# One decoder layer on one core: two groups of narrow matrix products issued as pairs in the two column halves of the TensorE array

## The chip, the cores and the metric

The kernel is one program on one core of one Trainium2 chip. The metric is the device time of one execution in microseconds. Before the change it is 1077.32 us, the median of three runs (1077.20 to 1079.56). All data and products are float32.

## What is computed

The reference is one hybrid decoder layer on x (256 tokens x 1024). What matters here is the compressed branch of the attention and the place where probabilities meet values:

```
# token mixer: one input projection; then attention (3 branches) beside a convolution branch
blocks = concat of two neighbouring chunks of 16 tokens, + pos_emb      # 15 blocks per group, 4 groups
kc = gelu(blocks.reshape(.., 32*96) @ w1k) @ w2k                        # w1k: 3072 x 256
vc = gelu(blocks.reshape(.., 32*64) @ w1v) @ w2v                        # w1v: 2048 x 256
o_cmp = softmax(q @ kc.T * scale + bias, masked) @ vc                   # 16 heads, value width 64
o_slc = softmax(q @ ks.T * scale + bias, causal) @ vs                   # all 4 blocks are selected
o_win = softmax(q @ kw.T * scale + bias, causal) @ vw
o = g0*o_cmp + g1*o_slc + g2*o_win                                      # -> w_attn_out, merged, w_out
# then PEER: q = h @ w_q; scores against sub-keys; top 16 of 128 x 128 experts for each of 8 heads;
# y = sum_e gelu(h . u[e]) * w_e * v[e]      (128 experts a token, rows u,v gathered from memory)
```

## The kernel before, in words

The program has one instruction stream per engine, written out by hand in the order of work; semaphores tie the streams together. TensorE executes its stream in order. Its stages are:

1. Input projection: `column_tile` multiplies 128x128 weight tiles by hT (channels x 256 tokens), 8 products per tile of output columns.
2. Block compression. Keys lie as kcA and kcB (first and second half of a block with position embedding; 96 rows of one position and 32 rows of another packed into 128 partitions) in `sc`, values as vcAB. For each of 24 steps the stationary operand is a slice of every 16th column of kcA or kcB (63 columns, one for each block of the four groups; NCG = 63) and the moving operand is a 128x256 slice of w1. All steps accumulate into `pb[0:63, 5, 0:256]`. ScalarE applies gelu into htok (63 x 256), and `hidden_transposed` turns it by two transposes into 128 x 63 twice. The values do the same in 16 steps into bank 7. In between and after stand the second layer products (w2k, w2v) and the first two tiles of the convolution's output projection (`conv_out`).
3. Attention: 32 units n, one for each of 2 token tiles (tt = 0, 1) and 16 heads. In each iteration TensorE runs `scores(n)`, some products of the convolution branch (`conv_pieces`, only while tt = 0), `transposes(n-2)` of the probabilities, and one piece of `values` of the group of four heads gi that was finished before; at every fourth iteration also `cmp_scores` and `cmp_transposes`. VectorE runs `logits(n)`, then `gated(n-1)`; ScalarE the exponentials and the copy of the turned probabilities into PT.
4. `values(gi, piece)`: the output of four heads lies in `o = pb[0:64, 6 + gi % 2, 0:512]` (64 value channels x 4 heads x 128 tokens). Piece 0 multiplies the compressed values vcv (15 rows x 64 columns) by PcT (15 x 512); the other products multiply V (128 x 64) by PT (128 x 512). With tt = 0 there are 1 + 2 products for a group, with tt = 1 there are 1 + 4. These are 8 products at L704 and 24 at L709. `attention_out(gi)` on ScalarE copies even heads to partitions 0-63 of hT and odd heads to partitions 64-127, with two instructions that each read 64 partitions, and each raises a_o by 1.
5. After the attention: `attention_out_half` (products by w_attn_out), `out_part` (by w_out), norms, the first query columns and sub-key scores, and the search for the first experts on VectorE.
6. Experts: GpSimd issues indirect DMAs of 256 rows a token tile and expert (1 MB each) at L516 as `rowat` places come free; VectorE forms the dot products (L1479), TensorE adds diag x row into PSUM (`expert_chunk`, L794). The last additions and the store end the program.

Each float32 product appears in the trace as two records of TensorE, each with its own weight load (PEld).

Of the kernel before, what the change touches and what calls it, by code (L numbers as in the profile page):

```python
# [26 lines left out]
ACT = mybir.ActivationFunctionType  # L27
AX = mybir.AxisListType.X

P = 128  # L30
# [3 lines left out]
TT = SEQ // P  # L34
HEADS = 16
GROUPS = 4
REP = HEADS // GROUPS
DQK = 96
DV = 64
CMP_L = 32  # L40
CMP_ST = 16
NCMP = SEQ // CMP_ST - 1
NBLK = SEQ // CMP_ST
NFAR = (P - CMP_L) // CMP_ST + 1
NCG = GROUPS * NBLK - 1
HID = 256
# [31 lines left out]
KAT = 8  # L78
# [111 lines left out]
def build(nc, a, out):  # L190
    ctx = ExitStack()
    with ctx:
        def sb(name, shape, dt=F32):
            return ctx.enter_context(nc.sbuf_tensor(name, shape, dt))

        def sem(name):
            return ctx.enter_context(nc.semaphore(name))
# [9 lines left out]
        w1 = arena[:, 4:12, :].rearrange("p a b -> p (a b)").rearrange("p (l n) -> p l n", n=HID)  # L207

        x = sb("x", [P, TT, D])
        hT = sb("hT", [P, DT, SEQ])  # L210
# [6 lines left out]
        V = sb("V", [P, TT, 2 * GROUPS * DV])  # L217
# [10 lines left out]
        sc = sb("sc", [P, 4096])  # L228
# [14 lines left out]


        kcA, kcB, vcAB = (sc[:, 1024 * i:1024 * i + 1024] for i in range(3))
        ssb = sc[:, :].rearrange("p (t m k) -> p t m k", t=TT, k=NK)
        pair = sb("pair", [P, 2 * D])
        S = pair[:, :].rearrange("p (u b t) -> p u b t", u=4, b=2)
# [5 lines left out]
        PT = arena[:, 4:8, :].rearrange("p a b -> p (a b)").rearrange("p (u k t) -> p u k t", u=2, t=512)  # L254
        scaled = [sc[:, 1024:2048], sc[:, 1024:2048]]
        spare = sb("spare", [P, 2 * D])
        PcT = spare[:, 1024:2048].rearrange("p (u t) -> p u t", u=2)
        htok = spare[0:NCG, 0:512].rearrange("p (u n) -> p u n", u=2)
        tbc = spare[:, 512:512 + TT * HEADS * NCMP].rearrange("p (t h n) -> p t h n", t=TT, h=HEADS)

        rowat = [qk[:, 3 * D:5 * D]]
# [17 lines left out]
        table = sb("table", [BUCKETS + 1, HEADS])  # L279
# [7 lines left out]
        vcv = sb("vcv", [NCMP, GROUPS * DV])  # L287
# [8 lines left out]
        ident = sb("ident", [P, P])  # L296
# [29 lines left out]
        pb = ctx.enter_context(nc.psum_tensor("pb", [P, 8, 512], F32))  # L326
# [15 lines left out]
        v_sc, v_p, v_pc, a_o = sem("v_sc"), sem("v_p"), sem("v_pc"), sem("a_o")  # L342
        g_const, g_rowok, g_chain = sem("g_const"), sem("g_rowok"), sem("g_chain")
        a_c, a_ss, a_std, a_rev = (sem(n) for n in ("a_c", "a_ss", "a_std", "a_rev"))
        a_evac, a_v, a_gk, a_hk, a_kc, a_gv, a_hv, a_vc, a_stdc, a_z = (
            sem(n) for n in ("a_evac", "a_v", "a_gk", "a_hk", "a_kc", "a_gv", "a_hv", "a_vc", "a_stdc", "a_z"))
# [28 lines left out]
        def group_of(gi):  # L375

            return divmod(gi, GROUPS)
# [145 lines left out]
        def _(pe):  # L523
            mm = nc.tensor.matmul
# [4 lines left out]
            for hf in range(2):  # L529
                last = mm(pb[:, hf, :], ones[0:1, :], crow[:, hf * 512:(hf + 1) * 512], start=True, stop=True)  # L530
# [3 lines left out]
            for j in range(DT):  # L534
                if j == 4:
                    pe.wait_ge(v_xs, TT)
                    for t in range(TT):
                        last = mm(pb[:, 2, t * P:(t + 1) * P], ones[:, :], turn[:, t, :], start=True, stop=True)
                    last.then_inc(p_xT, 1)
                for t in range(TT):  # L540
                    o = (j % 2) * SEQ + t * P
                    last = nc.tensor.transpose(pb[:, 4 + j // 2, o:o + P], x[:, t, j * P:(j + 1) * P], ident[:, :])
# [22 lines left out]
            for k in range(DT):  # L565
                pe.wait_ge(ring_in[k], 16)
                pe.wait_ge(a_hT, k + 1)
                for n in range(ROUND):
                    if k == 0 and n >= 6:
                        pe.wait_ge(a_xh, n - 2)  # L570
                    last = mm(pb[:, n, 0:SEQ], ring[:, k, n * P:(n + 1) * P], hT[:, k, :],
                              start=(k == 0), stop=(k == DT - 1))
# [34 lines left out]
            pe.wait_ge(a_pack, 6)  # L607
            for n in range(3 * CMP_L // 4):
                l = n // 3 * 4 + n % 3
                src = kcA if l < CMP_ST else kcB  # L610
                last = mm(pb[0:NCG, 5, 0:HID], src[:, l:l + (NCG - 1) * CMP_ST + 1:CMP_ST], w1[:, KAT + n, :],
                          start=(n == 0), stop=(n == 3 * CMP_L // 4 - 1))
                if n == KAT - 1:
                    last.then_inc(p_hk, 1)
            last.then_inc(p_hk, 1)
            def hidden_transposed(u, bank):
                for hh in range(2):
                    last = nc.tensor.transpose(pb[:, bank, hh * 64:hh * 64 + NCG], htok[:, u, hh * P:(hh + 1) * P],
                                               ident[0:NCG, 0:NCG])
                return last  # L620

            pe.wait_ge(a_gk, 1)
            hidden_transposed(0, 6).then_inc(p_tk, 1)

            pe.wait_ge(w1v_in, 32)
            for l in range(CMP_ST):
                last = mm(pb[0:NCG, 7, 0:HID], vcAB[:, l:l + (NCG - 1) * CMP_ST + 1:CMP_ST], w1[:, l, :],
                          start=(l == 0), stop=(l == CMP_ST - 1))
            last.then_inc(p_hv, 1)
            pe.wait_ge(a_hk, 1)  # L630
            pe.wait_ge(s_small, 64)
            for k in range(2):
                last = mm(pb[0:DQK, 6, 256:256 + NCG], w2k[:, k, :], hidk[:, k, 0:NCG], start=(k == 0), stop=(k == 1))
# [12 lines left out]
            for g in range(GROUPS):  # L646
                for k in range(2):
                    last = mm(pb[0:NCMP, 5, 256 + g * DV:256 + (g + 1) * DV], hidv[:, k, g * NBLK:g * NBLK + NCMP],
                              w2v[:, k, :], start=(k == 0), stop=(k == 1))
# [6 lines left out]
            def cmp_scores(gi):  # L656
                tt, g = group_of(gi)
                if gi >= 3:
                    pe.wait_ge(a_o, 2 * (gi - 2))
                for hh in range(REP):  # L660
                    last = mm(pb[:, 6 + (gi + 1) % 2, hh * NCMP:(hh + 1) * NCMP], qT[0:DQK, g * REP + hh, tt * P:(tt + 1) * P],
                              kcT[:, g * NBLK:g * NBLK + NCMP], start=True, stop=True)
                last.then_inc(p_cs, 1)
# [11 lines left out]
            def scores(n):  # L675
                tt, h, g, hh, keys = unit_keys(n)
                if n >= 2:
                    pe.wait_ge(v_mx, 2 * (n - 1))
                mm(pb[:, n % 2, 0:2 * keys], qT[0:DQK, h, tt * P:(tt + 1) * P], kT[0:DQK, g, 1:3, 0:keys],  # L679
                   start=True, stop=True).then_inc(p_s, 1)  # L680
# [14 lines left out]

            def values(gi, piece):
                tt, g = group_of(gi)
                o = pb[0:DV, 6 + gi % 2, :]
                if piece == 0:
                    pe.wait_ge(a_pct, gi + 1)  # L700
                    if gi >= 2:
                        pe.wait_ge(a_o, 2 * (gi - 1))
                    pe.wait_ge(v_cs, min(gi + 2, GROUPS * TT))
                    mm(o, vcv[:, g * DV:(g + 1) * DV], PcT[0:NCMP, gi % 2, :], start=True, stop=False)  # L704
                pe.wait_ge(a_pt, REP * (gi + 1))
                products = [(b, kb) for b in range(2) for kb in range(tt + 1)]
                mine = products[piece:piece + 1] if tt else products[piece - 1:piece] if piece else []
                for b, kb in mine:
                    last = mm(o, V[:, kb, (b * GROUPS + g) * DV:(b * GROUPS + g + 1) * DV],  # L709
                              PT[:, gi % 2, b * (tt + 1) + kb, :], start=False, stop=((b, kb) == products[-1]))  # L710
                    if (b, kb) == products[-1]:
                        last.then_inc(p_o, 1)

# [23 lines left out]
            for n in range(NU + 2):  # L737
                if n < NU:
                    if n % REP == 0:
                        cmp_scores(n // REP)  # L740
                    scores(n)
                conv_pieces(n)
                if n >= 2:
                    transposes(n - 2)
                if n < NU and n % REP == 2:
                    cmp_transposes(n // REP)
                if n >= REP + 2:
                    values((n - REP - 2) // REP, (n - REP - 2) % REP)
                if n == NU:
                    pe.wait_ge(a_o, 2 * GROUPS)  # L750
                    pe.wait_ge(v_zb, DT)
                    attention_out_half(0, 0)
                    attention_out_half(0, 1)
                if n == NU + 1:
                    pe.wait_ge(v_mx, 2 * NU)
                    attention_out_half(0, 2)
# [71 lines left out]
            for hf in range(2):  # L828
                for k in range(DT):
                    last = out_part(0, k, (hf,))  # L830
                last.then_inc(p_out, 1)
            pe.wait_ge(a_o, 2 * GROUPS * TT)
            for j in range(3):
                attention_out_half(1, j)
            h2_transposes(0)
# [36 lines left out]
        def _(act):  # L872
            fn = nc.scalar.activation
# [70 lines left out]
            fn(stdc[:, :], pb[:, 4, SEQ:2 * SEQ], ACT.Sqrt, bias=eps[:, :]).then_inc(a_stdc, 1)  # L944
            fn(turned[:, :], eps[:, :], ACT.Gelu_apprx_tanh).then_inc(a_turn, 1)
            act.wait_ge(p_hk, 2)
            fn(htok[:, 0, :], pb[0:NCG, 5, 0:HID], ACT.Gelu_apprx_tanh).then_inc(a_gk, 1)
            act.wait_ge(p_tk, 1)
            fn(hidk[:, :, 0:NCG], pb[:, 6, 0:P].rearrange("p (a b) -> p a b", a=2)[:, :, 0:NCG],
               ACT.Copy).then_inc(a_hk, 1)  # L950
# [4 lines left out]
            act.wait_ge(p_kc, 1)  # L955
            fn(kcT[:, :], pb[0:DQK, 6, 256:256 + NCG], ACT.Copy).then_inc(a_kc, 1)
            act.wait_ge(p_hv, 1)
            fn(htok[:, 1, :], pb[0:NCG, 7, 0:HID], ACT.Gelu_apprx_tanh).then_inc(a_gv, 1)
            act.wait_ge(p_tv, 1)
            fn(hidv[:, :, 0:NCG], pb[:, 5, 0:P].rearrange("p (a b) -> p a b", a=2)[:, :, 0:NCG],  # L960
               ACT.Copy).then_inc(a_hv, 1)
# [20 lines left out]
            def attention_out(gi):  # L982
                tt, g = group_of(gi)
                act.wait_ge(p_o, gi + 1)
                o = pb[0:DV, 6 + gi % 2, :].rearrange("p (a b t) -> p a b t", b=2, t=P)
                for odd in range(2):
                    fn(hT[odd * DV:(odd + 1) * DV, 2 * g:2 * g + 2, tt * P:(tt + 1) * P], o[:, :, odd, :],
                       ACT.Copy).then_inc(a_o, 1)

            for n in range(NU + 2):  # L990
                gi = n // REP
# [677 lines left out]
```

## Time and profile before

| what | value |
|---|---|
| median of three runs | 1077.32 us |
| span of the profiled execution (first to last instruction) | 1074.3 us |
| part of the median outside that span | 3.0 us |
| PE busy / DVE / ACT / POOL | 954.7 / 732.4 / 297.0 / 337.1 us |
| queue of the indirect DMAs | 292.59 MB, 67.0% of 16 engines' span |
| mean rate over the span | 336 GB/s |

The profile gives no time for its own execution beside the span; 1074.3 us of span stand against 1077.32 us of median, so 3.0 us lie around the span (start and end of the program), and differences of span are read as differences of time. Busy shares are averages over stages with different limits; the stretches in the rows below separate the stages. In a timeline, the first number is the start of a group of instructions, the second the time it was busy, and "x" the number of records.

### The profile page before, as it was taken

Reading aid. Unit: us, or ns where it says so; the run is one execution under the profiler, and the core shown is the slowest. Engines: PE = TensorE matmul, PEld = TensorE weight load, DVE = VectorE, ACT = ScalarE, POOL = GpSimd, SP = SyncE. Lnnn points to the kernel's source line nnn. Section 1 sums busy time; section 2 is a strip of 40 time slices with the busy share of each in tenths; the row PEclk is TensorE's granted clock in tenths of the full one; section 3 lists DMA queues with packets and bytes.
Section 4 is the critical chain, followed back from the end, with each engine's and each line's share of the span. In section 5 each row is a group of like instructions: output and inputs, shape, how many; then the busy total and the mean of one; then the engine's idle time right before and its main releaser. Section 6 shows DMA issues by size and latency. Waiting matters only on the chain.

```text
span 1074.3 us, 11042 instructions
## 1 busy us (share of the span) xinstructions
PE 954.7 (89%) x3303; PEld 567.7 (53%) x3303; DVE 732.4 (68%) x1933; ACT 297.0 (28%) x811; POOL 337.1 (31%) x325
## 2 busy tenths in 40 slices
PE   7999999999999999899999878787778777778786
PEld 5788888887644675565565433333333323333332
DVE  6699798734456149768748667767678667667554
ACT  3211122254456121523312312212322212212222
POOL 0101003021000015445435644455444454444430
PEclk9999999999999999999999987999889999999899
DMA  9967748886100809999999999999999999999994
GB/s 364 403 248 224 266 150 333 333 306 132 59 20 6 339 32 409 423 384 423 421 422 422 420 423 421 423 424 421 423 423 422 422 423 423 422 423 423 422 423 172
DMA packets 63290, 361.91 MB, mean 337 GB/s; under 512 B 7500, under 2 KB 8156, under 8 KB 30078
## 3 DMA queue, kind: packets, MB, share of 16 engines
q0 software_dynamic: 43280, 292.59, 67.0%
q1 hardware_dynamic: 19950, 68.61, 17.2%
q8 instruction: 27, 0.44, 0.2%
q14 instruction: 33, 0.27, 0.1%
HBM read 359.58 MB, written 1.59 MB: 336 GB/s over the span
## 4 chain that ended last, share of the span: by engine, by line
PE 49%; DMA 35%; DVE 8%; ACT 2%; POOL 2%; issue 2%; SPq 2%; ACTq 0%; POOLq 0%; DVEq 0%
DMA arena<-in_peer_uv,idx 21%; PE pb L553 18%; PE pb L794 14%; DMA ring<-in_peer_uv,idx 10%; DMA qk<-in_peer_uv,idx 2%; PE pb L709 2%; PE pb L679 2%; PE pb L722 2%; PE pb L732 2%; DVE arena L1479 2%; DMA arena<-in_w_ada 2%; PE pb L587 1%; PE pb L774 1%; POOL arena L516 1%; PE pb L823 1%
## 5 line engine op out<-in xcount | busy, mean ns | idle before, releaser
L794 PE MATMUL pb<-arena,sig 128*128 128x512 f32 x416 | 193.3, 616 | 22.4 <-ACT sig L1071 22.4
L794 PE MATMUL pb<-ring,sig 128*128 128x512 f32 x288 | 140.3, 633 | 29.4 <-ACT sig L1071 29.4
L553 PE MATMUL pb<-hT,ring 128*128 128x256 f32 x752 | 162.8, 379 | 0.5 <-ACT arena L899 0.5
L516 POOL DMA_INDIRECT arena<-in_peer_uv,idx x104 | 123.1, 1183 | 113.2 <-PE pb L794 93.1
L1479 DVE CUSTOM_DVE_ANT_0 arena<-arena,sig 128x1024 f32<-128x1024 f32 x104 | 124.4, 1223 | 44.6 <-DMA arena<-in_peer_uv,idx 44.1
L553 PEld LDWEIGHTS pb<-hT,ring 128*128 128x128 f32 x752 | 142.7, 190 | 21.1 <-ACT arena L899 1.7
L794 PEld LDWEIGHTS pb<-arena,sig 128*128 128x128 f32 x416 | 80.9, 197 | 128.9 <-issue 128.7
L1068 ACT ACTIVATE gl<-dot 128x4 f32<-128x4 f32 (+1 forms) x73 | 14.9, 205 | 413.4 <-DVE dot L1479 397.1
L516 POOL DMA_INDIRECT ring<-in_peer_uv,idx x72 | 88.2, 1225 | 91.8 <-PE pb L794 82.4
L1479 DVE CUSTOM_DVE_ANT_0 ring<-ring,sig 128x1024 f32<-128x1024 f32 x72 | 87.7, 1224 | 40.9 <-DMA ring<-in_peer_uv,idx 40.4
L794 PEld LDWEIGHTS pb<-ring,sig 128*128 128x128 f32 x288 | 56.9, 203 | 105.8 <-issue 105.7
L794 PE MATMUL pb<-qk,sig 128*128 128x512 f32 x160 | 81.5, 648 | 27.4 <-ACT sig L1071 27.3
L1199 DVE SCALAR_TENSOR_TENSOR y<-arena,cols,y x240 | 95.2, 474 | 0.0
L1071 ACT ACTIVATE sig<-ident,cf 128x128 f32<-128x128 f32 x256 | 82.8, 390 | 16.8 <-DVE cf L1483 16.8
L516 POOL DMA_INDIRECT qk<-in_peer_uv,idx x40 | 47.0, 1176 | 117.9 <-PE pb L794 64.7
L463 POOL DMA_DIRECT2D arena<-in_w_ada x32 | 17.1, 541 | 167.5 <-DVE modst L1147 131.3
L1479 DVE CUSTOM_DVE_ANT_0 qk<-qk,sig 128x1024 f32<-128x1024 f32 x40 | 49.4, 1235 | 28.8 <-DMA qk<-in_peer_uv,idx 28.2
L794 PEld LDWEIGHTS pb<-qk,sig 128*128 128x128 f32 x160 | 31.0, 201 | 69.5 <-issue 69.3
L1290 DVE CUSTOM_DVE_ANT_0 pair<-pb,arena 128x128 f32<-128x128 f32 (+1 forms) x64 | 20.3, 355 | 37.2 <-PE pb L679 34.8
L794 PE MATMUL pb<-pair,sig 128*128 128x512 f32 x44 | 26.2, 727 | 20.5 <-ACT sig L1071 20.5
L1147 DVE CUSTOM_DVE_ANT_0 arena<-arena,sc 128x1024 f32<-128x1024 f32 x32 | 37.9, 1223 | 8.9 <-DMA arena<-in_w_ada 8.3
L794 PE MATMUL pb<-hT,sig 128*128 128x512 f32 x72 | 38.3, 658 | 0.4 <-ACT sig L1071 0.4
(313 smaller groups left out, 1263.0 us busy)
## 6 DMA issues: line engine op xcount, KB each, us to landing
ring<-in_w_stream SPq DMA_DIRECT2D x79, 512.0 KB, 7.2
arena<-in_w_ada POOLq DMA_DIRECT2D x32, 512.0 KB, 11.7
arena<-in_w_ada SPq DMA_DIRECT2D x12, 512.0 KB, 11.7
arena<-in_w_stream SPq DMA_DIRECT2D x8, 512.0 KB, 6.6
arena<-in_w1k SPq DMA_DIRECT2D x6, 512.0 KB, 8.6
spare<-in_w_stream SPq DMA_DIRECT2D x6, 512.0 KB, 8.5
pair<-in_w_stream SPq DMA_DIRECT2D x5, 512.0 KB
sig<-in_w_ada SPq DMA_DIRECT2D x4, 512.0 KB, 14.8
```

Of the source, the lines that this page charges most:

```text
L516: nc.gpsimd.indirect_dma_start(out=rowat[PLACE[n]], out_offset=None, in_=a["peer_uv"], in_offset=bass.IndirectOffsetOnAxis(ap=idx[:, c, e: ...
L553: last = mm(pb[:, bank, 0:SEQ], w[:, k * P:(k + 1) * P], src[:, k, :], start=(k == 0), stop=(k == DT - 1))
L679: mm(pb[:, n % 2, 0:2 * keys], qT[0:DQK, h, tt * P:(tt + 1) * P], kT[0:DQK, g, 1:3, 0:keys], start=True, stop=True).then_inc(p_s, 1)
L709: last = mm(o, V[:, kb, (b * GROUPS + g) * DV:(b * GROUPS + g + 1) * DV], PT[:, gi % 2, b * (tt + 1) + kb, :], start=False, stop=((b, kb) ...
L722: last = mm(pb[:, MERGE_BANK[q], side * P:(side + 1) * P], tile_at[SLOT[tile]][:, k * P:(k + 1) * P], hT[:, k, t * P:(t + 1) * P], start=( ...
L732: last = mm(pb[:, 4, 0:SEQ], ring[:, SLOT[T_CO + j], k * P:(k + 1) * P], y[:, k, :], start=(k == 0), stop=(k == DT - 1))
L794: last = mm(pb[:, 4 + 2 * t + hf, :], diag[:, c % DEEP, e, :], rowat[PLACE[n]][:, D + hf * 512:D + (hf + 1) * 512], start=(i == 0 and e == ...
L1071: fn(diag[:, b, s, :], ident[:, :], ACT.Copy, scale=cf[:, b, s:s + 1]).then_inc(a_dg, 1)
L1147: V_.tensor_tensor_reduce(out=w[:, s, :], in0=w[:, s, :], in1=cact, scale=1.0, scalar=0.0, op0=ALU.mult, op1=ALU.add, accum_out=modst[:, s ...
L1199: ins = V_.scalar_tensor_tensor(out=y[:, j, :], in0=upad[:, j, k:k + SEQ], scalar=w, in1=y[:, j, :], op0=ALU.mult, op1=ALU.add)
L1290: V_.tensor_tensor_reduce(out=S[:, n % 4, b, 0:keys], in0=pb[:, n % 2, b * keys:(b + 1) * keys], in1=tb[:, h, SEQ - keys:SEQ], scale=-SCAL ...
L1479: V_.tensor_tensor_reduce(out=u, in0=u, in1=h2[:, c // CPT, :], scale=1.0, scalar=0.0, op0=ALU.mult, op1=ALU.add, accum_out=dot[:, c % DEE ...
```

## The change

The products of the two places become pairs. Compression: the slice takes 64 columns instead of 63, and each step becomes two products, one with the first 128 columns of w1 into partitions 0-63 and one with the last 128 into partitions 64-127 of the same bank, columns 0-127. The gelu then reads 128 x 128, and the hidden layer is turned by one transpose instead of two. Values: every product of 64 x 512 becomes two of 64 x 256, even heads into partitions 0-63 and odd heads into 64-127, and ScalarE copies them out with one instruction of 128 partitions; the waits on a_o count half as many.

```diff
+        kcBv = sc[:, 1024:3072]
-        htok = spare[0:NCG, 0:512].rearrange("p (u n) -> p u n", u=2)
+        htok = spare[:, 0:256].rearrange("p (u n) -> p u n", u=2)
...
-                src = kcA if l < CMP_ST else kcB
-                last = mm(pb[0:NCG, 5, 0:HID], src[:, l:l + (NCG - 1) * CMP_ST + 1:CMP_ST], w1[:, KAT + n, :],
-                          start=(n == 0), stop=(n == 3 * CMP_L // 4 - 1))
+                src = kcA if l < CMP_ST else kcBv
+                for hh in range(2):
+                    last = mm(pb[hh * 64:hh * 64 + 64, 5, 0:P], src[:, l:l + 63 * CMP_ST + 1:CMP_ST],
+                              w1[:, KAT + n, hh * P:(hh + 1) * P], start=(n == 0), stop=(n == 3 * CMP_L // 4 - 1))
...
             def hidden_transposed(u, bank):
-                for hh in range(2):
-                    last = nc.tensor.transpose(pb[:, bank, hh * 64:hh * 64 + NCG], htok[:, u, hh * P:(hh + 1) * P],
-                                               ident[0:NCG, 0:NCG])
-                return last
+                return nc.tensor.transpose(pb[:, bank, 0:P], htok[:, u, :], ident[:, :])
...
             for l in range(CMP_ST):
-                last = mm(pb[0:NCG, 7, 0:HID], vcAB[:, l:l + (NCG - 1) * CMP_ST + 1:CMP_ST], w1[:, l, :],
-                          start=(l == 0), stop=(l == CMP_ST - 1))
+                for hh in range(2):
+                    last = mm(pb[hh * 64:hh * 64 + 64, 7, 0:P], vcAB[:, l:l + 63 * CMP_ST + 1:CMP_ST],
+                              w1[:, l, hh * P:(hh + 1) * P], start=(l == 0), stop=(l == CMP_ST - 1))
...
             def values(gi, piece):
                 tt, g = group_of(gi)
-                o = pb[0:DV, 6 + gi % 2, :]
+                def sides(v, table, first, final):
+                    for odd in range(2):
+                        last = mm(pb[odd * DV:(odd + 1) * DV, 6 + gi % 2, 0:2 * P].rearrange("p (a t) -> p a t", t=P), v,
+                                  table.rearrange("k (a b t) -> k a b t", b=2, t=P)[:, :, odd, :], start=first, stop=final)
+                    return last
...
-                    mm(o, vcv[:, g * DV:(g + 1) * DV], PcT[0:NCMP, gi % 2, :], start=True, stop=False)
+                    sides(vcv[:, g * DV:(g + 1) * DV], PcT[0:NCMP, gi % 2, :], True, False)
...
-                    last = mm(o, V[:, kb, (b * GROUPS + g) * DV:(b * GROUPS + g + 1) * DV],
-                              PT[:, gi % 2, b * (tt + 1) + kb, :], start=False, stop=((b, kb) == products[-1]))
+                    last = sides(V[:, kb, (b * GROUPS + g) * DV:(b * GROUPS + g + 1) * DV],
+                                 PT[:, gi % 2, b * (tt + 1) + kb, :], False, (b, kb) == products[-1])
...
-            fn(htok[:, 0, :], pb[0:NCG, 5, 0:HID], ACT.Gelu_apprx_tanh).then_inc(a_gk, 1)
+            fn(htok[:, 0, :], pb[:, 5, 0:P], ACT.Gelu_apprx_tanh).then_inc(a_gk, 1)
...
             def attention_out(gi):
-                o = pb[0:DV, 6 + gi % 2, :].rearrange("p (a b t) -> p a b t", b=2, t=P)
-                for odd in range(2):
-                    fn(hT[odd * DV:(odd + 1) * DV, 2 * g:2 * g + 2, tt * P:(tt + 1) * P], o[:, :, odd, :],
-                       ACT.Copy).then_inc(a_o, 1)
+                fn(hT[:, 2 * g:2 * g + 2, tt * P:(tt + 1) * P],
+                   pb[:, 6 + gi % 2, 0:2 * P].rearrange("p (a t) -> p a t", t=P), ACT.Copy).then_inc(a_o, 1)
```

## Rows read from the trace of the kernel before

**Rows 1.** The page's chain that ended last, by engine.

```profile
PE 49%; DMA 35%; DVE 8%; ACT 2%; POOL 2%; issue 2%; SPq 2%; ACTq 0%; POOLq 0%; DVEq 0%
```

**Rows 2.** Busy time by stretch, attention to end, with granted clock and DMA share.

```profile
core 0: us, PE busy (x) PEld busy (x) DVE busy (x) ACT busy (x) POOL busy (x), PEclk, DMA share, GB/s
253.00:299.00 46.00, 43.97 (x210) 31.89 (x210) 25.07 (x144) 22.82 (x89) 0.00 (x0) 1.00 0.26 82
299.00:349.10 50.10, 48.50 (x186) 21.22 (x184) 31.19 (x144) 30.66 (x98) 2.04 (x4) 1.00 0.05 13
349.10:363.60 14.50, 14.50 (x83) 9.23 (x82) 1.98 (x5) 2.04 (x5) 0.15 (x1) 1.00 0.83 319
363.60:412.00 48.40, 48.05 (x285) 35.92 (x285) 22.39 (x76) 11.13 (x26) 6.25 (x7) 1.00 0.48 183
412.00:530.00 118.00, 113.99 (x445) 68.87 (x444) 89.75 (x241) 37.23 (x101) 56.52 (x46) 1.00 1.01 414
530.00:1074.00 544.00, 440.73 (x986) 193.70 (x984) 372.04 (x920) 130.44 (x356) 243.61 (x205) 0.93 0.98 410
```

**Rows 3.** What PE waited for from 224 to 412 us (total, times, longest).

```profile
PE pb L732 <- DVE arena L1254: 2.0, 2, 1.0
PE pb L692 <- DVE pair L1303: 1.3, 3, 0.6
```

**Rows 4.** Timeline of PE around one isolated product of the values.

```profile
302.46 0.38 PE L692 MATMUL pb<-ident,pair 128*128 128x128 f32 x2
302.77 1.07 PE L709 MATMUL pb<-arena,V 128*64 128x512 f32 x2
303.77 1.12 PE L679 MATMUL pb<-qk 96*128 96x512 f32 x2
```

**Rows 5.** Timeline at the end of the values: a stream of products.

```profile
359.05 1.07 PE L704 MATMUL pb<-spare,vcv 15*64 15x512 f32 x2
360.04 3.65 PE L709 MATMUL pb<-arena,V 128*64 128x512 f32 x8
363.62 7.41 PE L722 MATMUL pb<-hT,ring 128*128 128x128 f32 x64
```

**Rows 6.** The weight loads of the same stream.

```profile
360.04 0.19 PEld L709 LDWEIGHTS pb<-arena,V 128*64 128x64 f32 x2 [0.81 <-issue]
360.52 0.14 PEld L709 LDWEIGHTS pb<-arena,V 128*64 128x64 f32 x1 [0.29 <-issue]
363.62 0.97 PEld L722 LDWEIGHTS pb<-hT,ring 128*128 128x128 f32 x8 [0.81 <-issue]
```

**Rows 7.** Key compression (L611): weight loads and products, min/median/max ns.

```profile
L611 PEld LDWEIGHTS pb<-arena,sc x48: 183/184/205, 224.9 to 234.9; 128*63 128x63 f32 x48
L611 PE MATMUL pb<-arena,sc x48: 379/379/480, 224.9 to 235.1; 128*63 128x256 f32 x48
```

**Rows 8.** Timeline from the key compression to the value compression and on.

```profile
235.55 0.38 ACT L947 ACTIVATE spare<-pb 63x256 f32<-63x256 f32 x1 [6.27 <-PE pb L611]
235.98 0.33 PE L618 MATMUL pb<-ident,spare 63*128 63x63 f32 x2 [0.47 <-ACT spare L947]
236.24 7.17 PE L627 MATMUL pb<-arena,sc 128*63 128x256 f32 x32
243.34 0.55 PE L633 MATMUL pb<-hidk,w2k 128*96 128x63 f32 x4
```

**Rows 9.** Streams of short records: 15, 128 and 64 moving columns.

```profile
251.25 1.07 PE L648 MATMUL pb<-w2v,hidv 128*15 128x64 f32 x16
252.25 1.06 PE L661 MATMUL pb<-kcT,qk 96*128 96x15 f32 x8
300.60 1.06 PE L661 MATMUL pb<-kcT,qk 96*128 96x15 f32 x8
301.51 1.10 PE L679 MATMUL pb<-qk 96*128 96x512 f32 x2
350.07 3.84 PE L722 MATMUL pb<-hT,ring 128*128 128x128 f32 x32
353.75 0.60 PE L692 MATMUL pb<-ident,pair 128*128 128x128 f32 x4
```

**Rows 10.** One iteration with tt = 1: scores, gating on VectorE, transposes.

```profile
326.89 1.12 PE L679 MATMUL pb<-qk 96*128 96x512 f32 x2
328.94 0.73 DVE L1303 TENSOR_SCALAR pair<-pair,rz,gates 128x256 f32<-128x256 f32 x2
329.38 1.12 PE L679 MATMUL pb<-qk 96*128 96x512 f32 x2
330.35 0.60 PE L692 MATMUL pb<-ident,pair 128*128 128x128 f32 x4
```

**Rows 11.** ScalarE's copies in the attention, by shape: busy, mean ns, idle before.

```profile
L979 ACT ACTIVATE arena<-pb 128x256 f32<-128x256 f32 x16 | 6.0, 372 | 5.1 <-PE pb L692 5.1
L987 ACT ACTIVATE hT<-pb 64x256 f32<-64x256 f32 x16 | 5.9, 371 | 8.2 <-PE pb L709 8.0
```

More of the change, by code:

```diff
@@ L658, in cmp_scores @@
                 if gi >= 3:
-                    pe.wait_ge(a_o, 2 * (gi - 2))
+                    pe.wait_ge(a_o, gi - 2)
                 for hh in range(REP):
@@ L701, in values @@
                     if gi >= 2:
-                        pe.wait_ge(a_o, 2 * (gi - 1))
+                        pe.wait_ge(a_o, gi - 1)
                     pe.wait_ge(v_cs, min(gi + 2, GROUPS * TT))
-                    mm(o, vcv[:, g * DV:(g + 1) * DV], PcT[0:NCMP, gi % 2, :], start=True, stop=False)
+                    sides(vcv[:, g * DV:(g + 1) * DV], PcT[0:NCMP, gi % 2, :], True, False)
                 pe.wait_ge(a_pt, REP * (gi + 1))
@@ L749, in _ @@
                 if n == NU:
-                    pe.wait_ge(a_o, 2 * GROUPS)
+                    pe.wait_ge(a_o, GROUPS)
                     pe.wait_ge(v_zb, DT)
@@ L831, in _ @@
                 last.then_inc(p_out, 1)
-            pe.wait_ge(a_o, 2 * GROUPS * TT)
+            pe.wait_ge(a_o, GROUPS * TT)
             for j in range(3):
@@ L957, in _ @@
             act.wait_ge(p_hv, 1)
-            fn(htok[:, 1, :], pb[0:NCG, 7, 0:HID], ACT.Gelu_apprx_tanh).then_inc(a_gv, 1)
+            fn(htok[:, 1, :], pb[:, 7, 0:P], ACT.Gelu_apprx_tanh).then_inc(a_gv, 1)
             act.wait_ge(p_tv, 1)
```

## The prediction

> **What bounds the kernel now.** I read the chain of work that ended last first: half of it is PE and a third DMA [rows 1], so there are stages with different limits. The busy times by stretch separate them [rows 2]. Up to 412 us PE is the limit: it is busy 43.97 of 46.00 us, 48.50 of 50.10, 14.50 of 14.50 and 48.05 of 48.40, while DVE and ACT reach about 60% at most. The reader is to see that the DMA share there is 0.05 to 0.83. From 412 us on the DMA share is 1.01 and then 0.98, at 414 and 410 GB/s: the expert rows are gathered at full rate to the end. The gather can't become shorter by this change, but it begins when the PE stages ahead of it end. A microsecond that PE saves ahead of 412 us moves the whole gather forward by one, and one that it loses moves it back. Both edited places lie ahead of it, and PE hardly waits there: 2.0 us in all for the convolution merges and 1.3 us for the gated probabilities [rows 3].
>
> **How long one product takes now.** The records end with a tail that overlaps the next, so I use start to start. The isolated product of the values goes from 302.77 to 303.77 [rows 4]: 1.00 us for two records of 512 moving columns. In the stream at the end, 8 such records take 363.62 - 360.04 = 3.58 us [rows 5]. Two equations, 2r + s = 1.00 and 8r + s = 3.58, give r = 0.430 us a record and s = 0.14 us for entering or leaving the shape of 64 weight columns. The weight loads show what s is: inside the stream the next weights load while the current record runs (one load at 360.52, between the records), but the first load at 360.04 and that of the following 128-column product at 363.62 begin only with their own record, after 0.81 us of idle [rows 6]. So the array is already driven in a 64-column shape there, and changing the shape drains it. The change keeps the shape (64 weight columns), so s is paid as often as before. A record of 256 moving columns takes half of 0.430, 0.215 us; the compression's own rows agree, 10.2 us for 47 steps from its first to its last record, 0.217 us [rows 7].
>
> **Values.** There are 32 products (8 + 24). The last four of L709 are one stream; the 28 others are isolated, each between other shapes: the product of vcv has 15 rows and that of V 128, and from 359.05 to 360.04 the change between these two costs the same 0.99 us a product [rows 5]. After the change each product is four records of 0.215 us: A1, A2 into partitions 0-63 and B1, B2 into 64-127.
> - If the halves of the array don't work at the same time, a pair costs 4 x 0.215 + 0.14 = 1.00 us: nothing gained.
> - If they do, the stream is still in order: A2 must follow A1 in its half, B1 can start beside A2, B2 follows B1. An isolated pair then costs 3 x 0.215 + 0.14 = 0.785 us, 0.215 less. In a stream each further pair costs two records, so the last four take 9 x 0.215 + 0.14 = 2.08 us in place of 3.58, 1.50 less.
> Together 28 x 0.215 + 1.50 = 7.5 us. No row of before shows two column halves in use at once; the bounds are 7.5 us gained and, if each change of half costs a drain, 35 changes (28 in isolated pairs, 7 in the stream) x 0.14 = 4.9 us lost. If B's weights load late, with the 0.14 us uncovered, an isolated pair gains 0.075 and the whole about 2.1 + 0.5 = 2.6 us. I take 7.5, since the two weight loads that come together at 360.04 (0.19 us for both) show loads fast enough to run ahead of records of 0.215 us.
>
> The Trainium skill (TensorEngine Tiling, "Key Properties") says that tiles run independently and that changing the tiling mode, not the tile, drains the engine. The drains at shape changes in the trace agree with the second half; no row here shows the first. The same skill (TensorE: Matmul & The Clock Gate, "Packing small matmuls") says that a weight load overlaps a running product only when the row group differs; here the trace disagrees, since the load at 360.52 runs under a product of the same rows, and the measurement decides. By that rule alone the values would gain nothing and the time would be that of the second rival below, 1077.7 us; the tiling page's rule gives the forecast.
>
> How much of it passes through: with tt = 1 the scores of an iteration follow those of the one before by 329.38 - 326.89 = 2.49 us, and the gated probabilities are ready at 328.94 + 0.73 = 329.67 while their transposes start at 330.35 [rows 10]. With 0.14 us for the weight load that leaves about 0.5 us of cover, more than the 0.215 taken from the iteration. In the iterations without a value piece PE waits already, and they gain nothing, but they have nothing to lose either. I pass 95%: 7.1 us. If the cover were gone, the loss would show as more wait at L692.
>
> **Compression.** Before: 24 key steps of two records. After: 96 records of 128 moving columns, each with a load of 64 weight columns taken at every 16th column. Those loads are slow: 183 ns for 63 columns [rows 7], where V's 64 neighbouring columns take about 0.14 us in the rows of the stream [rows 6]. Loads of 128 columns bind the stream of L661, whose moving operand is only 15 columns: 8 records from 300.60 to 301.51, 0.114 us each [rows 9]. L722, with 128 moving and 128 weight columns, needs 3.68 us for 32, 0.115 us [rows 9]. So I expect 0.108 to 0.115 us a record whether or not the products overlap, because the loads follow one another: 96 x 0.112 = 10.75 us against 48 x 0.217 = 10.4 now, 0.3 lost, and 64 x 0.112 = 7.2 against 32 x 0.217 = 6.9 in the value compression [rows 8], 0.2 lost. Bounds: if loads of different halves run side by side, two records of 0.108 make a pair's time and it gains half: 5.2 + 3.5 = 8.7 us less at most. If each change of half drains, 47 + 31 changes x 0.14 = 10.9 us more. I take +0.5, nearest to the two rows of streams with short records.
>
> **Small parts.** The gelu of the keys stands in PE's way: 0.38 us for 63 x 256, then PE starts at 235.98, having waited 0.47 [rows 8]. Half the free size makes it some 0.1 us shorter; one transpose in place of two about 0.05 (236.24 - 235.98 = 0.26 for both now). That of the values is hidden by `conv_out`. ACT's copies out of the values become one of 128 x 256 instead of two of 64 x 256; a 128-partition copy of that size takes 372 ns and each of 64 partitions 371 [rows 11], so 8 x 0.37 = 3.0 us of ACT go. ACT has slack there (30.66 of 50.10 us [rows 2]), so 0. The waits on a_o come at the same points. No DMA is added or moved; those that start on p_hk and p_o start that much earlier or later with PE.
>
> **Sum.** -7.1 + 0.5 - 0.15 = -6.8 us. Span 1074.3 - 6.8 = 1067.5; with the 3.0 us between the span and the median of the runs 1070.5 us.
>
> **The rivals.**
> - Both overlap, loads too. For it: nothing in the rows ties the loads of one half to the other. Against: each of PE's loads in the rows stands behind the one before. Time: a pair of compression records is unlikely to reach the bound of 8.7 us fully; at the 0.063 us a record that the shortest stream of the values' second layer needs (16 records from 251.25 to 252.25 us [rows 9]) it is 96 x 0.063 = 6.0 and 64 x 0.063 = 4.0, so 4.4 + 2.9 = 7.3 less. With the values 7.1 and 0.15: -14.5, 1062.8 us.
> - The change doesn't do what it says: float32 products of the two halves run one after the other. For it: every record in the trace follows the one before with no overlap in the array. Values 0, compression +0.5, small -0.15: 1077.7 us, up to 1078.6 if a record there takes 0.12 us.
> - The other side: every change of the column half drains as a change of shape does, 0.14 us. For it: the exposed loads of [rows 6]. Against: what changes there is the number of columns, not only where they are. It decides from the first pair on. 4.9 + 10.9 + 0.5 - 0.15 = +16.1: 1093.5 us; if it does so only in the values or with half the price, 1082 to 1086.
>
> **How the numbers follow.** Forecast (values overlap, compression bound by loads) 0.40, with 1069 to 1075 as its own range; both overlap 0.20; no overlap 0.26; drains 0.14. Less than 0.3% (3.2 us) can't be told from no change here. Faster: 0.20 + 0.37 of the forecast's 0.40 = 0.57. Same: 0.03 + 0.23 = 0.26. Slower: 0.14 + 0.03 = 0.17. The range reaches from the second case to the serial one and a part of the drains: 1061 to 1080.5.
>
> **What would show it.** In the profile after, the starts of L709's successor: a pair of four records with 128x256 should take 0.79 us to the next shape's start, 1.00 if serial, 1.14 if it drains. The last stream before L722 should take 2.1 us. The key compression should take 10.4 to 11.0 us from first to last record; 6 us would show parallel loads, 17 us drains. L692's waits should stay below 3 us in all. From 412 us on the stages should be only shifted: DMA share 0.98 and over. If the PE stages end earlier and the end doesn't move, the gather was bound to something else, and that would make the prediction wrong.

## The result

The changed kernel takes 1063.76 us, the median of four runs (1061.19 to 1066.58), against 1077.26 us; the ratio is 0.9871, 95% interval 0.9846 to 0.9896, or 13.5 us less. A second series of runs of it gave 1063.99 us and 0.9876 (0.9861 to 0.9891). I had forecast 1070.5 us, 6.8 less. The sign was right, the size half of the measured one, and two of the steps were wrong in opposite directions.

The profiled execution has a span of 1064.8 us, 9.5 less than the 1074.3 before, and its time, 1066.58 us, is the longest of the first four. The span gained 4.0 us less than the median. In every run with a time and a span of its own on record the time is 1.7 to 1.9 us more than the span, so the profiled execution before took about 1076.1 us (an estimate, 1074.3 + 1.8), 1.2 less than its median, and the profiled one after took 2.8 more than its median: 13.5 - 1.2 - 2.8 = 9.5. These are the milestones of the two traces:

| start of | before | after | gained since the row above |
|---|---|---|---|
| key compression (L611, now L613) | 224.89 | 226.75 | -1.86 |
| its transposes (L618, L619) | 235.98 | 232.95 | 4.89 |
| value compression (L627) | 236.24 | 240.85 | -7.64 |
| second layer of the keys (L633) | 243.34 | 246.11 | 1.84 |
| first scores of the attention (L661) | 252.25 | 254.66 | 0.36 |
| products after the last values (L722, L729) | 363.62 | 353.79 | 12.24 |
| w_out (L774, L781) | 370.87 | 361.04 | 0.00 |
| end of the span | 1074.3 | 1064.8 | -0.3 |

The code ahead of the first row is the same in both. In the traces of this case the key compression starts anywhere from 224.8 to 228.1 us, so the 1.86 us are not put down to the change; what they come from is open. Everything from the last values on is only shifted. The lengths of stages, compared over all traces at the end of the experiments, don't suffer from the different starts.

**Values.** This is PE's timeline of the changed kernel around the same isolated product as in [rows 4]; L702 now stands for L704 and L709.

```profile
301.52 0.38 PE L692 MATMUL pb<-ident,pair 128*128 128x128 f32 x2
301.83 0.65 PE L702 MATMUL pb<-arena,V 128*64 128x256 f32 x4
302.41 1.13 PE L679 MATMUL pb<-qk 96*128 96x512 f32 x2
```

From 301.83 to 302.41 the pair takes 0.58 us, where the product took 1.00. Two record times of 0.215 and the drain of 0.14 make 0.57: four records in the time of two. The same pair, cut to what started before 302.00, and its weight loads:

```profile
301.83 0.44 PE L702 MATMUL pb<-arena,V 128*64 128x256 f32 x2
```
```profile
301.83 0.20 PEld L702 LDWEIGHTS pb<-arena,V 128*64 128x64 f32 x4 [0.17 <-issue]
```

Two records are there, and together they are busy for 0.44 us, about as long as one of them alone (up to 430 ns, the first of a stream has the longest tail). The rows don't name the half of a record. But two records of one half follow each other by a record time (experiment 3), so the two that start together are A1 and B1, not A1 and A2. All four weight loads are done in 0.20 us. The stream at the end, against [rows 5]:

```profile
351.33 0.65 PE L702 MATMUL pb<-spare,vcv 15*64 15x256 f32 x4
351.91 1.95 PE L702 MATMUL pb<-arena,V 128*64 128x256 f32 x16
353.79 7.41 PE L729 MATMUL pb<-hT,ring 128*128 128x128 f32 x64
```

16 records take 1.88 us (before: 8 records, 3.58).

**Compression.** Timeline of PE, and the durations of the key compression's records (min/median/max ns), against [rows 7, 8]:

```profile
226.75 5.82 PE L613 MATMUL pb<-arena,sc 128*64 128x128 f32 x96
232.95 0.33 PE L619 MATMUL pb<-ident,spare 128*128 128x128 f32 x1 [0.38 <-ACT spare L954]
240.85 5.32 PE L627 MATMUL pb<-arena,sc 128*64 128x128 f32 x64 [7.58 <-DMA arena<-in_w1v]
246.11 0.55 PE L633 MATMUL pb<-hidk,w2k 128*96 128x63 f32 x4
```
```profile
L613 PEld LDWEIGHTS pb<-arena,sc x96: 188/198/221, 226.7 to 232.2; 128*64 128x64 f32 x96
L613 PE MATMUL pb<-arena,sc x96: 274/277/380, 226.7 to 232.3; 128*64 128x128 f32 x96
```

96 records in 5.8 us, 0.060 us each. The slow loads last 198 ns each, a little more than the 184 of [rows 7], and yet one is done every 0.060 us: the loads of the two halves run side by side as well. But then PE waits 7.58 us for the second half of w1v. GpSimd's timeline and the stretches (the last three numbers are granted clock, DMA share, GB/s) show why:

```profile
229.20 0.53 POOL L471 DMA_DIRECT2D arena<-in_w1v  x1 [16.57 <-PE pb L613]
233.20 8.41 POOL L477 DMA_DIRECT2D arena<-rev_scratch  x16 [3.47 <-PE pb L613]
```
```profile
229.00:233.00 4.00, 3.62 (x64) 3.43 (x61) 3.31 (x2) 2.38 (x5) 0.53 (x1) 1.00 1.04 420
233.00:241.00 8.00, 0.42 (x3) 0.23 (x5) 0.88 (x2) 5.60 (x10) 7.80 (x15) 0.76 1.03 215
241.00:246.00 5.00, 5.00 (x64) 4.99 (x64) 0.00 (x0) 0.00 (x0) 0.60 (x2) 0.70 1.05 161
```

The transfer is issued when the first 8 key steps free their place, at 229.20; it lands 11.6 us later, at about 240.8. From 233.20 on GpSimd issues the 16 copies of the bias table, and in the stretch that follows the DMA share stays at 1.03 while the rate falls from 420 to 215 GB/s. Before it was issued at 228.9, landed after 6.5 us at 235.4, and was used at 236.24: 0.8 us of slack that I had not looked for. While PE idles the granted clock falls, to 0.76 and 0.70 in the mean of these stretches, which mix full and half speed (2.4 and 1.2 GHz); the value compression begins in it and takes 5.3 us; in experiment 4, with no wait and at the full clock, it takes 4.0.

**The rest.** What PE waited for from 224 to 412 us, against [rows 3], and the gather's stretches, against [rows 2]:

```profile
PE pb L627 <- DMA arena<-in_w1v: 7.6, 1, 7.6
PE pb L739 <- DVE arena L1259: 2.0, 2, 1.0
PE pb L692 <- DVE pair L1308: 2.0, 3, 0.8
```
```profile
404.00:530.00 126.00, 121.99 (x461) 72.90 (x461) 97.12 (x258) 41.01 (x112) 60.37 (x49) 1.00 1.00 413
530.00:1064.00 534.00, 423.93 (x954) 185.13 (x952) 362.75 (x899) 126.64 (x344) 236.07 (x201) 0.94 0.98 410
```

The gather runs at the same rate and is only earlier.

### The profile page after: what moved, and what is told of

Read it like the earlier page. It is cut to its first block, busy times and chain, and to the rows that moved or that the text cites. A ratio compares the mean times of both kernels' runs of the same rounds, so it can differ in the third digit from the quotient of the medians.

```text
span 1064.8 us, 11318 instructions
## 1 busy us (share of the span) xinstructions
PE 928.2 (87%) x3445; PEld 561.7 (53%) x3445; DVE 731.9 (69%) x1933; ACT 293.6 (28%) x803; POOL 335.0 (31%) x325
## 4 chain that ended last, share of the span: by engine, by line
PE 51%; DMA 37%; DVE 6%; ACT 2%; SPq 2%; issue 2%; POOL 1%; POOLq 0%; ACTq 0%; DVEq 0%
DMA arena<-in_peer_uv,idx 19%; PE pb L554 18%; PE pb L801 16%; DMA ring<-in_peer_uv,idx 15%; PE pb L781 3%; PE pb L729 2%; PE pb L739 2%; DMA arena<-in_w_ada 2%; PE pb L679 2%; PE pb L830 2%; DVE arena L1484 1%; PE pb L588 1%; PE pb L702 1%; DMA arena<-in_w1v 1%; DVE ring L1484 1%
## 5 line engine op out<-in xcount | busy, mean ns | idle before, releaser
L801 PE MATMUL pb<-arena,sig 128*128 128x512 f32 x416 | 193.4, 616 | 27.6 <-ACT sig L1076 27.6
L801 PE MATMUL pb<-ring,sig 128*128 128x512 f32 x288 | 137.2, 620 | 30.7 <-ACT sig L1076 30.7
L517 POOL DMA_INDIRECT ring<-in_peer_uv,idx x72 | 85.4, 1186 | 91.8 <-PE pb L801 81.7
L801 PE MATMUL pb<-hT,sig 128*128 128x512 f32 x72 | 35.5, 617 | 0.4 <-ACT sig L1076 0.4
```

The source lines that it names most:

```text
L517: nc.gpsimd.indirect_dma_start(out=rowat[PLACE[n]], out_offset=None, in_=a["peer_uv"], in_offset=bass.IndirectOffsetOnAxis(ap=idx[:, c, e: ...
L801: last = mm(pb[:, 4 + 2 * t + hf, :], diag[:, c % DEEP, e, :], rowat[PLACE[n]][:, D + hf * 512:D + (hf + 1) * 512], start=(i == 0 and e == ...
```

## The experiments

All times are medians against the kernel before on the same chip.

**1. The compression alone as pairs**, values as before (the diff of the change without `values` and `attention_out`).

> Only the compression as pairs, the values as before. Theory (records of the two halves start within some ns of each other, and the weight loads of the two halves run side by side too; the second half of w1v then arrives late and gives part back): key compression from first to last record 5.5 us in place of 10.2, value compression 3.8 to 5.3 in place of 6.8, but PE waits 3 to 8 us for w1v ahead of the latter. Time 0 to 5 us below before. Rival (the gain of the compression is whole and the time in the two is lost nowhere): 7 to 8 us below before.

Measured: 1076.01 against 1077.04 us, ratio 0.9986 (0.9978 to 0.9995), 1.0 us. PE's timeline:

```profile
226.94 5.82 PE L613 MATMUL pb<-arena,sc 128*64 128x128 f32 x96
240.20 5.76 PE L627 MATMUL pb<-arena,sc 128*64 128x128 f32 x64 [6.75 <-DMA arena<-in_w1v]
```

The theory holds for the time: nearly all that the two compressions gain goes into the wait. The value compression takes 5.7 us, more than the 3.8 to 5.3 expected; its first 4.1 us lie at a granted clock of 0.50.

**2. The values alone as pairs**, compression as before.

> Only the values as pairs (and the one copy of 128 partitions), compression as before. Theory: an isolated product takes 0.58 us start to start in place of 1.00, so 28 x 0.42 + 1.7 = 13.4 us less of PE time, some of it turning into waits for VectorE: span of attention 12 us shorter, time 11.5 to 12.5 us below before, and no wait for w1v, since the key compression takes its 10.2 us. Rival (much of the gain of the whole change comes from the compression): 7 us below before.

Measured: 1064.06 us, ratio 0.9877 (0.9862 to 0.9891), 13.0 us, a little more than the theory's 12.5. No wait for w1v. Experiments 1 and 2 add up to 14.0, the whole change gives 13.5: the measured gain is that of the values.

**3. The same narrow products, both of a pair in one half of the array** (abridged; the compression keeps its 63 weight columns).

```diff
-                last = mm(pb[0:NCG, 5, 0:HID], src[...], w1[:, KAT + n, :], ...)
+                for hh in range(2):
+                    last = mm(pb[0:NCG, 5, hh * P:(hh + 1) * P], src[...], w1[:, KAT + n, hh * P:(hh + 1) * P], ...)
...
+                        last = mm(pb[0:DV, 6 + gi % 2, :].rearrange("p (a b t) -> p a b t", b=2, t=P)[:, :, odd, :], v, ...)
```

> The same narrow products (64 weight columns x 128 or 256 moving) in both places, but both of a pair into partitions 0 to 63, side by side in the bank; copies and gelu as before. Theory (the gain is that two halves of the array work at once): no overlap, values 1.00 us a pair as before, compression bound by its slow weight loads at 0.108 to 0.12 us a record, so 10.4 to 11.5 and 7 to 7.7 us; time 0 to 2 us above before. Rival (short records overlap in any place, or a narrower product is cheaper by itself): time 5 to 13 us below before.

Measured: 1077.37 us, ratio 1.0003 (0.9995 to 1.0012). The key compression, and a pair of the values with what follows it:

```profile
228.04 10.76 PE L612 MATMUL pb<-arena,sc 128*63 128x128 f32 x96
...
357.77 1.08 PE L705 MATMUL pb<-arena,V 128*64 128x256 f32 x4
358.77 3.84 PE L733 MATMUL pb<-hT,ring 128*128 128x128 f32 x32
```

The pair takes 1.00 us, the key compression 10.76 and the value compression 7.2. Narrower or shorter records give nothing; it is the second half of the array. The prediction's price of a serial record, 0.112 us, is met here.

**4. w1v early**: the changed kernel, with the second half of w1v loaded into a quarter of `sc` and half of `pair`, both free at that time (GpSimd's part of the edit; TensorE waits for all three transfers and reads the last eight steps from the two places).

```diff
-            g.wait_ge(p_hk, 1)
-            g.dma_start(w1[:, KAT:CMP_ST, :], a["w1v"][:, KAT:CMP_ST, :]).then_inc(w1v_in, 16)
             g.wait_ge(rev_out, 16)
+            for i in range(2):
+                g.dma_start(w1v_late[i], a["w1v"][:, KAT + 4 * i:KAT + 4 * i + 4, :]).then_inc(w1v_in, 16)
```

> The changed kernel with the second half of w1v loaded early into two places that are free (no wait for the first 8 key steps, 2 DMAs of 512 KB in place of one of 1 MB). Theory (the late w1v costs the changed kernel 7.6 us of wait, and some more by the clock that falls to 1.2 GHz in it): no wait ahead of the value compression, which takes 3.8 us or less at the full clock; 7 to 9 us below the changed kernel's profiled span of 1064.8, so 1056 to 1058 of span, 1058 to 1060 of time. Rival (the gather's start is bound by something else behind the attention, or the copies of the bias, which wait for the end of the key compression, come too late in turn): no more than 3 us below 1063.8.

Measured: 1058.40 us (1055.71 to 1059.97), ratio 0.9817 (0.9801 to 0.9834), 18.6 us below before. The whole compression runs through; 96 and 64 records:

```profile
228.00:233.90 5.90, 5.89 (x97) 5.61 (x96) 2.87 (x2) 4.42 (x10) 0.00 (x0) 1.00 1.03 410
234.50:238.40 3.90, 3.90 (x65) 3.85 (x64) 0.79 (x2) 3.75 (x7) 3.90 (x8) 1.00 1.02 266
```

The span, 1056.7 us, is 8.1 below the changed kernel's, as expected; the medians differ by 5.4, since that kernel's profiled execution was 2.8 us above its median. It beats both kernels.

**5. The changed kernel again**, for a second profile. No line of it differs.

> The changed kernel once more, for a second profile: its first runs fell into two groups, 1061.3 and 1066.4 us. Theory (what differs is how late the second half of w1v lands behind the other transfers): the wait ahead of the value compression is 2 to 8 us and differs from the 7.6 us of the first profile by as much as the times do. Rival (the start of the program differs, as the first records of the input projection at 45.6 us against 43.8 in the kernel before suggest): the wait is 7 to 8 us again and the times go with the start of the projection.

Measured: 1063.99 us (1062.31 to 1065.17), ratio 0.9876. The wait was 6.35 us, the landing 10.4; the span was 1063.4, 1.4 shorter. The wait was 1.2 us shorter, but the values' compression took 6.1 us instead of 5.3, more of it at the low clock (5.1 us against 3.2 at 0.50), which gave most of that back. The key compression started 0.5 us earlier (226.26 against 226.75), the first scores 0.9, and the other 0.5 us come behind them. So neither theory is confirmed, and the two groups of the first four runs remain unexplained; here the runs didn't form them.

**6. and 7. How far apart partners may stand.** On top of experiment 4, the order of the compression's products: n products of the first half, then n of the second (one line of the edit; n is RUN_K for the keys and RUN_V for the values). Each was run once: 1058.06 us with runs of 2 and 4, 1071.4 with runs of 24 and 16. In the second the granted clock was 0.50 from 308 to 321 us, in the attention, so its time isn't used; the stages below lie ahead of that.

```diff
+            for hh, n in [(hh, b + i) for b in range(0, 3 * CMP_L // 4, RUN_K) for hh in range(2) for i in range(RUN_K)]:
```

> Kernel of the early w1v, with another order in the compression: two products of the first half, then two of the second (keys), four and four (values' compression). Theory A (each half of the array has its own place in the queue, so that a product finds its partner some products away): keys 5.8 us and values 3.9 us from first to last record, as with alternating products. Theory B (TensorE starts records in the order of the program, and only neighbours overlap): a run of 4 records of the one half overlaps only at its edge, 6 of 8 record times for the keys, 8.1 us, and 14 of 16 for the values, 6.3 us.

> As e6, with all 24 key products of the first half ahead of all 24 of the second, and 16 and 16 for the values. Theory A with a short queue, and theory B: no overlap but at one edge, keys 10.4 to 10.8 us, values 6.9 to 7.3 us, at 0.108 to 0.112 us a record. Theory A with a long queue: 5.8 to 8 us for the keys.

| products in a run | records | us (keys: busy; values: to the next stage's start) |
|---|---|---|
| keys, 1 (changed kernel) | 96 | 5.8 |
| keys, 2 | 96 | 5.9 |
| keys, 24 | 96 | 10.7 |
| values' compression, 1 (experiment 4) | 64 | 4.0 |
| values' compression, 4 | 64 | 5.1 |
| values' compression, 16 | 64 | 7.0 |

Theory A would give 5.8 and 3.9 us in runs of 2 and 4, theory B 8.1 and 6.3; the keys go with A, and the values, at 5.1, lie between the two. TensorE does reach past products of a busy half, but not far. Where the run of 16 changes halves (operand `pair` is the end of the first half, `arena` the start of the second), the second half's first record starts at 242.13, 0.44 us, or four record times, ahead of the point where it runs alone:

```profile
242.13 0.38 PE L630 MATMUL pb<-arena,sc 128*64 128x128 f32 x1
242.23 0.27 PE L630 MATMUL pb<-pair,sc 128*64 128x128 f32 x1
242.34 0.28 PE L630 MATMUL pb<-arena,sc 128*64 128x128 f32 x1
242.34 0.28 PE L630 MATMUL pb<-pair,sc 128*64 128x128 f32 x1
242.45 0.28 PE L630 MATMUL pb<-arena,sc 128*64 128x128 f32 x1
242.46 0.27 PE L630 MATMUL pb<-pair,sc 128*64 128x128 f32 x1
242.57 1.62 PE L630 MATMUL pb<-arena,sc 128*64 128x128 f32 x13
```

Here the operands tell the two halves apart: records of `arena` start ahead of records of `pair` that come before them in the program. The order of the program, which the description of the kernel before took for the order in TensorE, holds within a half.

**8. The kernel before with w1v early.**

> The kernel before, with the second half of w1v loaded early into the free places, nothing else. Theory (before, w1v landed at 235.4 us, 0.8 us ahead of its use, so that it cost nothing): within 0.1% of before. Rival (the early place of the transfer helps by itself, by what it takes out of the way of the bias copies): 2 us or more below before.

Measured: 1077.27 us, ratio 1.0005 (0.9996 to 1.0014). The profiled execution, 1081.65 us, had a granted clock of 0.50 from 310 to 320 us. The early place is worth something only once the compression is fast.

**9. The bias copies only when w1v has landed**: the changed kernel with one line more, so that the 16 copies of small packets don't meet the transfer.

```diff
             g.wait_ge(p_hk, 2)
+            g.wait_ge(w1v_in, 32)
```

> The changed kernel with one more wait: the 16 copies of the bias table (issued from the end of the key compression on, in small packets) are issued only when w1v has landed. In the changed kernel w1v takes 10.4 and 11.6 us to land and PE waits 6.3 and 7.6 us for it. Theory (the copies, now issued 3 us earlier against w1v, share the DMA engines with it and delay it): w1v lands in about 7 us, as the 6.5 us before the change, the wait is 3 to 4 us, and the time is 1060 to 1062 if the bias still comes in time for the first scores. Rival (w1v queues behind the weight tiles that were issued before it, and the copies don't matter): it lands in 10 us or more, the wait is as long as before, and the time 1063 to 1066.

Measured: 1061.52 us (1061.22 to 1061.71), ratio 0.9858 (0.9842 to 0.9874). w1v lands in 7.4 us, and PE waits 3.3:

```profile
236.28 5.51 PE L628 MATMUL pb<-arena,sc 128*64 128x128 f32 x64 [3.31 <-DMA arena<-in_w1v]
```

As the theory had it: of the 6.3 and 7.6 us of wait, some 3 to 4 come from the copies that start earlier and share the engines, and 3.3 are there because the value compression now wants its weights sooner than a transfer issued at 228.9 can bring them. With the wait added the median is about 2 us lower. The intervals of the two ratios overlap, and two of the eight runs of the changed kernel (1061.19 and 1061.34) are as fast as these four, so the trace, where the way to the first scores is 3.7 to 4.1 us shorter, is the stronger evidence.

**The stages over all traces.** Here are the lengths, in us, from the start of the key compression to the first scores, from there to the products after the last values, and from the first product of w_out to the end of the span:

| trace | compression | attention | w_out and experts |
|---|---|---|---|
| before; experiment 8 | 27.4; 27.4 | 111.4; 116.2 (clock) | 703.4; 703.1 |
| experiment 3, one half | 27.6 | 111.5 | 703.7 |
| experiment 1, compression as pairs | 27.5 | 111.4 | 703.0 |
| experiment 2, values as pairs | 27.4 | 99.1 | 703.8 |
| changed; experiment 5 | 27.9; 27.5 | 99.1; 99.1 | 703.8; 703.3 |
| experiment 9, bias copies later | 23.9 | 99.1 | 703.3 |
| experiment 4, w1v early | 19.0 | 99.1 | 703.3 |
| experiments 6; 7 | 20.2; 26.8 | 99.1; 104.6 (clock) | 703.1; 703.4 |

"(clock)" marks the two traces with a stretch at half clock in the attention. The values as pairs are worth 12.2 to 12.4 us in all others, the pairs in the compression nothing as long as w1v is late and 8.4 with it early. The medians show 5.4 of the last figure and not the 8.6 to 9.0 by which the traces of experiment 4 and of the changed kernel differ here; both traces of the changed kernel are of executions above its median (by 2.8 and 1.2 us), and what the faster ones did differently isn't known.

## Why the prediction was half right

- **What bounds the kernel, and that PE time ahead of the gather counts one for one**: right. The gain at the last values (9.83 us) is that at w_out (9.83), and the span's is 9.5. In all eleven traces the part from w_out to the end takes 703.0 to 703.8 us.
- **The 3.0 us between span and time**: too much. It set one execution's span against the median of others; where both are known they are 1.7 to 1.9 us apart. With 1.8 the same sum would have given 1069.3 us; the difference between before and after doesn't hang on it.
- **The drain s = 0.14 us and the record of 0.215**: right; 0.58 and 1.88 us follow from them with two records a pair.
- **Values, "the stream is still in order: A2 must follow A1 in its half, B1 can start beside A2"**: wrong, and the costliest step. B1 starts beside A1 (two records busy for 0.44 us together), so an isolated pair costs two record times, not three: 28 x 0.42 + 1.70 = 13.5 us of PE time in place of the 7.5 that I had called the upper bound, and the attention became 12.24 us shorter in place of 7.1. I let the order of the program stand for the order in the array. The runs of 2 products (experiment 6) show that TensorE goes past waiting records of one half to those of the other.
- **95% passes through**: 12.24 of 13.5, 91%. Setting the two traces side by side record by record shows the 1.2 us. The three waits at L692 rose by 0.18, 0.09 and 0.42 us. Twice the transposes of the compressed probabilities (L672) came 0.25 us later against the work ahead of them, since VectorE had not finished Sc:

```profile
325.80 0.47 PEld L692 LDWEIGHTS pb<-ident,pair 128*128 128x128 f32 x4 [0.56 <-DVE pair L1308]
326.58 0.33 PEld L672 LDWEIGHTS pb<-ident,Sc 128*15 128x15 f32 x4 [0.32 <-DVE Sc L1317]
```

Together these are 1.2 us. The prediction had looked for lost cover at L692 alone.
- **Compression, "the loads follow one another"**: wrong. 5.8 and, without the stall, 4.0 us, where 10.75 and 7.2 were forecast. Experiment 3 shows that the price was right for one half of the array; with two halves a record costs about half of it. I had this as a rival at 0.20.
- **"No DMA is added or moved"**: the sentence was true and the conclusion lacking. The wait on p_hk fixes when w1v starts, and a faster compression wants it sooner, while the bias copies start earlier and collide with it (experiment 9). That took back 7.64 us in the profile, more than the 6.7 that the two compressions gained. The profile before had the warning: landing at 228.9 + 6.5 = 235.4, use at 236.24.
- **ACT's part at 0, small parts 0.15**: no run changes the copies alone, and the account of the values above leaves nothing for them. The wait for the gelu of the keys fell from 0.47 to 0.38 us. From the end of the value compression to the first scores 0.36 us more were gained than I counted, all of it around the second transposes (0.10 ahead of them, 0.15 in them, 0.11 behind), which now have the 128x128 shape of their neighbours.

The rival "both overlap, loads too" gave 1062.8 us and the measurement 1063.8, but that is no credit to it: it had 7.1 us from the values (measured 12.2 in the trace, 13.0 in the time) and 7.3 from the compression (measured 1.0 in the time). Its two errors nearly cancelled, which is luck.

Not tried: the same pairs with other element types, and four quarters of the array instead of two halves.

## What to carry to other kernels

Two float32 products of 64 weight columns that are neighbours in the program cost here as much time as one of them when their outputs lie in partitions 0-63 and 64-127, weight loads included; keep partners next to each other. Before a stage is made faster, list the transfers that are released in it or just ahead of it, with landing and first use: here the slack was 0.8 us, the faster stage waited 6.3 to 7.6, and moving the transfer was worth 5 us of median. When a transfer is late, look also at what else is released by the same faster stage. Traces of two executions are best compared by the lengths of their stages: the same code began up to 3.3 us apart here.

## What the runs showed of the hardware

- Records of the two column halves start within the same hundredth of a microsecond, and slow loads (64 columns, every 16th element, 198 ns) then finish one every 0.060 us; in one half it is one every 0.112 us.
- The reach past records of a busy half is about four records: full overlap with runs of 2 products, partial with 4 (5.1 us, where alternation takes 4.0 and one half 7.2), a single edge with 16 and 24.
- The Trainium skill (TensorE: Matmul & The Clock Gate, "Packing small matmuls") describes matrix products as strictly in order and column groups as running together with a few nanoseconds between starts. The second is what the trace shows: two records begin at 301.83, and at 242.34 one of each half. The first doesn't hold between the halves here: in experiment 7 a record of the second half starts at 242.13, ahead of three of the first half that precede it in the program (242.23 to 242.46), and the measurement decides. With float32's two records to a product it is this that gives A1, B1, A2, B2 and the whole gain.
- After waits of 3.3, 6.3, 6.7 and 7.6 us on PE (experiments 9, 5, 1 and the changed kernel) the value compression took 5.4, 6.1, 5.7 and 5.3 us instead of 4.0. It goes not with the length of the wait but with the time that the granted clock was at 0.50 while it ran: 3.4, 5.1, 4.1 and 3.2 us.
